# Where the filler products stand in two hand-ordered attention loops

## What is computed

```python
# MoBA, with one block of 256 keys: causal attention, per head
l_own = jnp.where(kpos[None, :] <= qpos[:, None], q @ k.T, -jnp.inf)
o = softmax(l_own) @ v                     # v = rmsnorm(x) @ w_v, 8 heads x 128

# second block, each of two layers
y_conv = conformer_conv(u_val, u_gate, ...) @ w_pw2 * silu(g_conv)   # g_conv = h @ w
y_attn = dsa_attention(...) * silu(g_attn)
y = concatenate([y_conv, y_attn], axis=-1) @ w_out[l]
x = x + gate * rmsnorm_2(y, g_post[l])
```

## Time and profile before

| | us |
|---|---|
| median of 3 runs | 949.56 |
| lowest, highest | 948.84, 949.63 |
| the profiled execution | 948.84 |
| its span in the trace | 947.0 |
| PE busy in it | 936.0 |
| DVE busy | 799.8 |
| ACT busy | 278.2 |

### The profile page before, as it was taken

How to read it: one execution, slowest core, us unless ns; L and a number is a source line. 1 busy time by engine, 2 the same in 40 slices (tenths; PEclk the granted TensorE clock), 3 DMA queues, 4 the chain that set the end, 5 groups by cost and what they waited for, 6 DMA issues and landing times.

```text
span 947.0 us, 16131 instructions
## 1 busy us (share of the span) xinstructions
PE 936.0 (99%) x6456; PEld 865.2 (91%) x6456; DVE 799.8 (84%) x1822; ACT 278.2 (29%) x622; POOL 0.7 (0%) x7
## 2 busy tenths in 40 slices
PE   9999999999999999999999999999999999999997
PEld 7888999999999998889999999999888878888876
DVE  4778879999998878777699999988799985899953
ACT  1033122221212111263122221220424563624561
POOL 0000000000000000000000000000000000000000
PEclk9999999999999999999999999999999999999999
DMA  8942455363634650757254545446933428443101
GB/s 312 411 184 105 178 187 218 153 254 147 264 140 160 231 209 3 282 195 305 94 224 171 230 180 221 181 161 241 341 133 98 159 94 297 156 149 110 32 1 45
DMA packets 36859, 171.80 MB, mean 181 GB/s; under 512 B 5032, under 2 KB 8880, under 8 KB 23344
## 3 DMA queue, kind: packets, MB, share of 16 engines
q1 hardware_dynamic: 35120, 167.72, 47.7%
q10 hardware_dynamic: 1664, 3.04, 0.9%
HBM read 169.69 MB, written 2.64 MB: 182 GB/s over the span
## 4 chain that ended last, share of the span: by engine, by line
PE 92%; DVE 3%; DMA 2%; ACT 1%; issue 0%; ACTq 0%; SPq 0%; DVEq 0%
PE bank L1355 26%; PE bank L1375 15%; PE bank L1039 9%; PE bank L1458 5%; PE bank L1692 4%; PE bank L1108 3%; PE bank L1331 3%; PE bank L1301 3%; PE bank L1115 3%; PE bank L1678 3%; PE bank L1554 2%; PE bank L1573 2%; PE bank L1051 1%; PE bank L1498 1%; PE bank L1624 1%; DMA ring<-in_ring 1%
## 5 line engine op out<-in xcount | busy, mean ns | idle before, releaser
L1375 PE MATMUL bank<-work,fring 128*128 128x128 f32 x1008 | 115.5, 275 | 0.0
L1375 PEld LDWEIGHTS bank<-work,fring 128*128 128x128 f32 x1008 | 114.0, 192 | 0.0
L2514 DVE SCALAR_TENSOR_TENSOR work<-work,cols 128x256 f32<-128x256 f32 x240 | 98.8, 477 | 1.0 <-ACT work L893 0.5
L1355 PE MATMUL bank<-sq,fring 128*128 128x128 f32 x640 | 84.5, 275 | 0.0
L724 ACT ACTIVATE work<-work,cols 128x256 f32<-128x256 f32 x88 | 47.8, 593 | 111.0 <-DVE work L2237 96.2
L1355 PE MATMUL bank<-ring,fring 128*128 128x128 f32 x640 | 78.1, 275 | 0.0
L1355 PE MATMUL bank<-sq,ring 128*128 128x128 f32 x640 | 78.0, 275 | 0.0
L1355 PEld LDWEIGHTS bank<-sq,fring 128*128 128x128 f32 x640 | 77.9, 192 | 0.0
L1355 PEld LDWEIGHTS bank<-ring,fring 128*128 128x128 f32 x640 | 74.8, 192 | 0.2
L1355 PEld LDWEIGHTS bank<-sq,ring 128*128 128x128 f32 x640 | 74.7, 192 | 0.0
L2256 DVE SCALAR_TENSOR_TENSOR work<-work,cols 128x256 f32<-128x256 f32 x176 | 71.5, 477 | 0.0
(11 more groups left out here) (420 smaller groups left out, 1724.7 us busy)
## 6 DMA issues: line engine op xcount, KB each, us to landing
ring<-in_ring SPq DMA_DIRECT2D x60, 1024.0 KB, 6.9
fring<-in_up SPq DMA_DIRECT2D x44, 1024.0 KB, 6.8
ada_w<-in_ada SPq DMA_DIRECT2D x48, 512.0 KB, 6.3
fring<-in_down SPq DMA_DIRECT2D x44, 512.0 KB, 4.5
ring<-in_ring SPq DMA_DIRECT2D x2, 800.0 KB, 6.5
bias_skewed<-bias_rows SPq DMA_DIRECT2D x1, 1536.0 KB, 13.1
consts<-in_consts ACTq DMA_DIRECT2D x1, 1128.0 KB, 15.2
ring<-in_ring SPq DMA_DIRECT2D x2, 512.0 KB, 4.6
```

Source lines behind the costliest of these rows:

```text
L1355: last = mm(bank[:, P * at:P * (at + 1)], w[:, k, P * c:P * (c + 1)], x[:, k, :], start=(k == 0), stop=(k == 3))
L1375: last = mm(bank[:, at + P * c:at + P * (c + 1)], w[:, P * c:P * (c + 1)], x, start=(i == 0 and at == 0 and c == 0), stop=(i == FF_STEPS - 1),
L2514: marks[c] = link(v.scalar_tensor_tensor(b_y[:, c, :], b_a[:, c, tap:tap + T], col("conv_w_2", 124 * l + 4 * tap + c), b_y[:, c, :], ALU.m ...
```

## The change

Two places in PE's stream change; DVE, ACT and SP keep their text.

In MoBA's attention parts 2 and 3 of the values both go into step 1, parts 4 to 7 into steps 2 to 5, and step 6 is left with no part. The waits for load 27 and for bank 7, which stand ahead of part 4, go with it from step 3 to step 2. The signals behind parts 3 and 7 come in steps 1 and 5.

In the layers' attention k-step 4 of `mix(0, 0, ...)` goes from step 8 to step 7, ahead of step 7's `mix(0, 1, 5, 6)`, and with it the wait for the second `gates_cp`. Step 8 keeps k-step 5. This happens once in each of the two layers.

```diff
@@ values(n), MoBA
-                for q in ((0, 1) if n == 0 else (n + 1,) if n < 7 else ()):
+                for q in ((0, 1) if n == 0 else (2, 3) if n == 1 else (n + 2,) if n < 6 else ()):
                     i, b, half = q // 4, q // 2 % 2, q % 2
@@ layer(l), steps 7 and 8
                     elif i == 7:
+                        pe.wait_ge(S("gates_cp"), 2 * l + 2)
+                        mix(0, 0, 4, 5)
                         pe.wait_ge(S("y2_attn"), 4 * l + 2)
                         mix(0, 1, 5, 6)
                     elif i == 8:
-                        pe.wait_ge(S("gates_cp"), 2 * l + 2)
-                        mix(0, 0, 4, 6)
+                        mix(0, 0, 5, 6)
```

## The result

Six executions of the changed kernel gave a median of 953.63 us (951.88 to 955.82) against 949.41 us for the kernel before: the ratio is 1.0042, with a 95% interval of 1.0025 to 1.0058. So the kernel became slower, as forecast, but by 4.2 us where 2.3 was named, and 0.4 us beyond the range given. Three of those six executions lie at 951.9 to 952.5 and three at 954.8 to 955.8; executions 1.9 to 4.4 us above the median come with the kernel before too (11 of its 90), and whether the change has a part in their number here stays open. Over all executions of this study the medians are 951.98 (27 of the changed kernel) and 949.52 (90 of the kernel before), 2.46 us apart.

What follows compares the result with a forecast made beforehand. PE's stream plus its few gaps was taken to bound the kernel, with matmul work unchanged. MoBA's +1.23 and 0.55 per layer summed to 2.33 us, on a base of 949.34: 951.7 us, range 950.1 to 953.2.

Steps and rivals of the forecast that it cites:

- MoBA, step 1: Two parts run without a gap before the transposes in MoBA's step 1; the next scores come 1.28 us later.
- MoBA, step 6: Without its part, PE's transposes wait for DVE's scaling, 0.49 us from scaling to PE; step 6 gives back only 0.05 us.
- The layers: Step 7's filler waits for ACT's gate copy; through ACT's chain step 8's transposes come 0.55 us later in each layer.
- 0.05 after a wait: Layers' step 7: extra time of the moved k-step behind its wait, estimated at 0.05 us.
- the step into the pair product: Layers' step 7: extra time before the pair product starts, taken as 0.09 us with bounds 0 and 0.18.
- the same rows: Layer 1, steps 7 and 8: timeline taken to match layer 0's, with a delay of 0.55 us.
- The sum: Whole kernel: 1.23 us in MoBA plus 0.55 in each of two layers, 2.33 us slower.
- (a): Layers' delay is free if step 7's transposes come less than 0.79 us later; 950.6 us, chance 0.11.
- (b): Layer 0's delay is swallowed behind that layer, where DVE waits for a DMA; 951.1 us, chance 0.10.
- (c): MoBA's step 6 has no wait on the scaling and gives back 1.72 us; 950.0 us in all, chance 0.06.
- (d): Granted clock falls in MoBA's new gap of 1.65 us, costing another 9.7 us; 961.4 us, chance 0.03.
- unseen costs of some tenths at each of three waits: At the three waits: the reason given for extending the range upward, to 953.2 us.

Runs made afterwards that it cites:

- layers_only: Only the layers' half of the change, against the kernel before: 951.73 us, ratio 1.0026.
- layers_swapped: The layers' half alone, with step 7's moved k-step and its wait behind the other k-step, against the kernel before: 950.74 us, ratio 1.0008.
- all_early: The kernel before with all six remaining parts of the values in MoBA's step 1, none in steps 2 to 6: 957.57 us, ratio 1.0085.
- dummy_fill: The changed kernel with four k-steps of unused matmul where MoBA's step 6 lost its part: 952.18 us, ratio 1.0039 to the kernel before.
- filled start: The changed kernel with six idle matmul pairs where PE waits for the input tiles: 953.11 us, ratio 1.0040 to the kernel before.
- bare start: The changed kernel without the four idle matmul pairs PE starts with: 951.87 us, ratio 1.0026 to the kernel before.

## Why the prediction was right and where it was wrong

**What bounds it, and the mechanisms: right.** Only gaps came, no work. Every step named was seen: no wait in step 1, a wait on the scaling in step 6, a wait on L862 in step 7 of both layers, none in front of the pair product, and step 8's transposes still waiting, at the end of a chain that now starts at PE.

**MoBA, step 1: right.** The next scores come 5.09 us after the loop's start (409.32 to 414.41). Before, they came 3.80 after it (408.70, and 412.50 in the earlier trace rows). That is +1.29 for 1.28. The loop's start before:

```profile
408.70 0.39 PE L1405 MATMUL bank<-work 128*128 128x128 f32 x2
```

**MoBA, step 6: right in kind, off by 0.07.** The transposes started 0.41 us behind the last scaling (429.69 to 430.10), not 0.49. The release latency was taken from the one wait that the trace of before has, in step 1, and it was 0.08 too long there. All five traces in which step 1 has its short wait show 0.49 or 0.50 there, and every wait of 1.40 in the others shows 0.40 or 0.41, so it goes with the wait and is no accident; its cause stays open. The step behind the wait took 0.05 longer (430.10 to 430.48 is 0.38, against 0.33) where 0.02 was named. Step 6 gave back 0.12 in place of 0.05, and MoBA cost 1.17 in place of 1.23.

**The layers: right in kind, small by 0.08 each.** From the filler's start to the pair product it took 766.83 - 764.90 = 1.93 us, and 0.91 + 0.86 + 0.09 = 1.86 had been named. The term that was too small is the 0.05 after a wait. The same two k-steps without a wait reach the pair product in 1.82 (764.09 to 765.91 in the swapped kernel), which is twice 0.86 and 0.10, so the 0.09 for the step into the pair product was about right, and the wait cost 0.11. The single starts say the same: behind the wait the second matmul starts 0.32 after the first, and each later one 0.22 after the last. From copy to scaling it was 0.39 for 0.37. The delay of 0.63 lies within the bounds given, 0.46 to 0.64.

Layer 1 does not have quite "the same rows", as the prediction says. Its filler of step 7 started 0.33 ahead of the gate copy (902.97 and 903.30), where in layer 0 it was 0.04, and its pair product then waited 0.31 for ACT. After the change its filler waits 0.79 and not the 0.6 that was named as a sign; the pair product's own wait is gone. The sum did not suffer, since it starts from the copy's end in both layers.

**The sum: right.** 2.33 was forecast, 2.43 is in the stages, and 2.46 between the medians of all executions. Some of that closeness is luck, as MoBA came out 0.06 lower and the layers 0.16 higher.

**The rivals.** (a) is excluded by layers_only, and layers_swapped shows its decision point at work: a delay of 0.64 at step 7's transposes costs nothing, since it stays below 0.79. (b) fell: DVE starts behind that DMA 2.69 us later than before (783.71 to 786.40), its wait there grew from 1.57 to 1.81, and PE's 0.7 stayed. The stretch between the layers was 108.56 in both profiled executions. That equality alone would prove little, as the stretch lies anywhere from 108.27 to 109.11 in the eight traces of the changed kernel, but their mean is 108.67. (c) fell by the wait itself, and by all_early five times over. (d) fell: in the trace the granted clock is 1.00 behind the gap of 1.4 us (430 to 441 us), and behind five of them.

**The time and the range: wrong.** The step that failed is the upper bound of the range: the term for the scatter of the executions themselves, which the prediction put at nothing. It named only "unseen costs of some tenths at each of three waits" as a reason to go higher, and allowed 1.5 us above its forecast of 951.7, though it wrote that 1.9 us of difference can come from no change at all. Its three executions of before lay within 0.8 us of one another. But 11 of 90 executions of the kernel before lie above 951.1, up to 953.9, and 5 of 27 of the changed kernel above 953.5. The base was sound: 949.34 was taken, and 949.41 and 949.52 were measured. In the first six executions of the changed kernel there were three upper ones. They pulled the median from 952.0 to 953.63, beyond the upper end of 953.2; that is some 1.6 of the 1.9 us by which the forecast of the time was off. A range for a median of a few executions had to hold that case.

**What stays open.** What the upper executions are. Of the 16 just counted nine have a mean granted clock of 0.997 and seven 0.998 to 1.000. That mean says little about PE's products: in all 18 kept traces the recorded clock is below full only behind PE's last product, in the last 0.4 to 3.6 us of the span (for the kernel before, the first line is the time up to there, the second the end).

```profile
0.00:943.00 943.00, 935.99 (x6456) 865.23 (x6456) 798.33 (x1820) 278.16 (x622) 0.69 (x7) 1.00 0.49 182
943.90:947.00 3.10, 0.00 (x0) 0.00 (x0) 0.60 (x2) 0.00 (x0) 0.00 (x0) 0.50 0.48 169
```

(In such a line the busy times of PE, its weight loads, DVE, ACT and POOL are followed by the granted clock, here 1.00 and 0.50, and the DMA columns.) A mean of 0.997 would be some 5 to 7 us at half the clock, an estimate from the rounded mean. They may lie under products, or in an end that is longer than the 6.1 us which all traces have from the start of PE's last product on. That last case, time lost behind PE's work, was not tested. The upper executions don't need the change's gap in MoBA (dummy_fill), nor a bare or a filled start as far as the two kernels tell. No trace holds one. The first set may be chance: if 5 such executions fall at random among 27, three or more of them land in a given six about once in 18 times, and the other 21 hold only two. A part of the change in it, on so few executions, can't be excluded.

## What to carry to other kernels

Filler between two waits is worth what it hides: before moving it, find what ends the wait that will stand in its place, and whether that release hangs on work that PE issued just before. Here 1.72 us of matmuls hid a wait of 1.6 us on DVE, and taking them away saved 0.1. Put first what is ready and second what waits: the same k-step cost 0.63 us ahead of its neighbour and nothing behind it. And before trusting a median of six to a tenth of a per cent, measure how far many executions of the unchanged kernel scatter; three that agree don't show it.

## What the runs showed of the hardware that was not expected

Stages bound by PE repeat from one execution to the next: the stretch from MoBA's loop to layer 0, with some 2300 matmuls, took 302.54 to 302.58 us in all 18 traces, on several chips. So a change of 0.1 us can be read from two traces although the whole time scatters by 2 us and more.

The granted clock that the profile prints for the first microseconds is no measurement. In the kernel before, matmuls start 0.43 us apart up to 5.10 us and 0.22 apart behind it; in the bare start the pace doubles at 9.74. The views print 1.00 on either side, as for the bare start:

```profile
4.00:9.70 5.70, 5.49 (x12) 4.04 (x13) 1.65 (x6) 2.28 (x4) 0.00 (x0) 1.00 0.88 270
9.80:14.00 4.20, 4.20 (x21) 3.71 (x20) 3.76 (x7) 0.63 (x1) 0.00 (x0) 1.00 0.91 280
```

The clock record in the two traces begins at 5.17 and at 9.75 us, just where the pace doubles, and the views count what lies ahead of it as full. By the pace, the products ahead of it ran at the lower of the clock's two levels.
